# Sixteen gate tiles of the mix made between the steps of inversion, scan and latent attention

## Chip, core and metric

The program runs on one core of a Trainium2 chip. The metric is the device time of one execution in microseconds; the time before is 2737.14 us, the median of three runs (2735.2 to 2739.61).

## What is computed

Two blocks on 256 tokens (16 meta tokens more in the first), width 2048, fp32. The first block is a differential attention and a pooling mixer. The second normalises h, multiplies it by one wide matrix and splits the result in three:

```python
u = rms_norm_2(h, pre_mix_norm[i])
z = u @ w_in[i]
z_rw, z_mla, z_gate = jnp.split(z, (RW_COLS, RW_COLS + MLA_COLS), axis=-1)
y_rw = rwkv7_mixer(z_rw, ...)
y_mla = mla_mixer(z_mla, ...)
g_rw, g_mla = jnp.split(jax.nn.sigmoid(z_gate), 2, axis=-1)
mix = (g_rw * (y_rw @ w_branch_rw[i]) + g_mla * (y_mla @ w_branch_mla[i])) @ w_out[i]
h = h + rms_norm_2(mix, post_mix_norm[i])
```

The gate columns z_gate are 2 x 2048; they depend on u alone. In `rwkv7_mixer` k is multiplied by k_k and divided by the root of its sum of squares per head; `rwkv7_scan` is a recurrence over the tokens for 16 heads of 64. `mla_mixer` is an attention with 8 heads over blocks of 128 queries. After the mix come a feed-forward part (5632 wide, with a convolution) and a gated embedding.

## The kernel before

All activations stand transposed: channels on 128 partitions, tokens along the row, so a 2048-wide tensor is 16 tiles of 128 x 256 (`KT`). Weights stream from DRAM in **slots** of 1 MB (4 x 512 columns on 128 partitions); `SLOTS_OF` gives their order, 393 in all. Four slots are in SBUF at a time (`RAW`). SP asks for slot n as soon as PE is done with slot n-4 (semaphore `slot_used`, `load_weights` L232). Each fp32 product is made of three fp32r products: ScalarE casts a slot to its high part (`split_hi`, L184), VectorE subtracts to get the low part (`split_lo`, L198), each in two halves, and `products` (L208) multiplies high by high, high by low and low by high (L220, L221, L222). `products` waits for `lo_done`. A slot is 48 products of 128 x 128 by 256 columns. A slot is split about two slots before PE uses it. PSUM is eight banks of 512 columns.

Every engine has its order written out by hand; `then_inc` and `wait_ge` on named semaphores hold them together.

The recurrent mixer (`rw_pe` L1060, `rw_act`, `rw_pool`, `rw_dve`) does the heads in two halves b. Per half: 14 slots give k, then w and a (a small slot), r, the gate g (slot n+9, small) and v. VectorE takes each from PSUM with the token shift (`shifted`, L1047 to L1054), sums the logs of the decay in six levels (L1376, L1377), and inverts the norm of k in two reciprocals (L1385, L1387). POOL scales k by k_k and squares it (L1310, L1312). Then come the **grams** (L1127, L1135: 64-wide products of chunks), their masks on VectorE (L1414 to L1425), the **inversion** of a triangular matrix per chunk in five **levels** (L1148 with POOL's mask L1330, ScalarE's copy L1272, then L1157 and L1158, and VectorE's sums L1433, L1434), the **turning** (transposes L1165 and ScalarE's copies, L1173), and the **scan** over four chunks x (L1184, L1190, L1195, L1201, L1202, L1206, L1207), in which `sa` goes through ScalarE (L1282), and the state and `pb` through VectorE (L1458, L1460, L1451). Behind it head sums (L1069) start the group norm while the products of the next part run. The scan stage streams no weights.

`mla_pe` (L1497) does attention per head: `turned` (three transposes of the probabilities), `scores` of head h+2, `values` of head h-1. VectorE takes maxima, divides and takes the low part of the output; ScalarE makes the exponentials.

`mix_pe` (L1745) runs four turns k of 12 slots: 4 for g_rw, 4 for g_mla, 2 for each branch; `mix_dve` multiplies the gates by the norm's factor `rs`, ScalarE takes the sigmoid, VectorE multiplies by the branch and adds both. A gate tile there takes 16 contraction tiles, as everywhere.

## Time and profile before

| what | value |
|---|---|
| median of three runs | 2737.14 us |
| the profiled execution, its own time | 2738.05 us |
| its span, first to last instruction | 2736.3 us |
| mean granted TensorE clock | 0.955 |
| PE busy | 2571.3 us (94%) |
| VectorE / ScalarE / POOL busy | 1653.5 (60%) / 1183.2 (43%) / 144.8 us (5%) |
| chain that ended last: PE / VectorE / ScalarE / POOL | 85% / 8% / 3% / 2% |
| lines L220, L221, L222 in that chain | 26%, 25%, 25% |

PE's busy time counts matmuls whose ends are modelled, so a busy PE is not PE at its peak. The granted clock is 1.00 at 2.4 GHz and 0.50 at 1.2 GHz. An instruction's idle time is put down to whoever released it last.

### The profile page before, as it was taken

Reading aid. Unit: us, or ns where it says so; the run is one execution under the profiler, and the core shown is the slowest. Engines: PE = TensorE matmul, PEld = TensorE weight load, DVE = VectorE, ACT = ScalarE, POOL = GpSimd, SP = SyncE. Lnnn points to the kernel's source line nnn. Section 1 sums busy time; section 2 is a strip of 40 time slices with the busy share of each in tenths; the row PEclk is TensorE's granted clock in tenths of the full one; section 3 lists DMA queues with packets and bytes.
Section 4 is the critical chain, followed back from the end, with each engine's and each line's share of the span. In section 5 each row is a group of like instructions: output and inputs, shape, how many; then the busy total and the mean of one; then the engine's idle time right before and its main releaser. Section 6 shows DMA issues by size and latency. Waiting matters only on the chain.

```text
span 2736.3 us, 52352 instructions
## 1 busy us (share of the span) xinstructions
PE 2571.3 (94%) x22506; PEld 2523.0 (92%) x22506; DVE 1653.5 (60%) x1896; ACT 1183.2 (43%) x1614; POOL 144.8 (5%) x85
## 2 busy tenths in 40 slices
PE   7999999999999887977988999999999999999997
PEld 7999999889999886977977999989999999999997
DVE  6556666565564884483464555548666666666675
ACT  5445455453444631331334333455444444444463
POOL 0000000005200031121000000000000000000000
PEclk9999999899999998797897999999999999999999
DMA  5444434344555430230331555544555555555443
GB/s 222 153 155 145 153 139 149 127 141 173 182 187 190 165 129 14 78 139 2 108 123 68 189 188 188 185 170 170 186 186 184 184 184 184 184 184 184 169 154 123
DMA packets 60053, 420.02 MB, mean 154 GB/s; under 512 B 6512, under 2 KB 8688, under 8 KB 9616
## 3 DMA queue, kind: packets, MB, share of 16 engines
q1 hardware_dynamic: 59712, 417.26, 42.7%
q8 instruction: 112, 1.84, 0.3%
q0 software_dynamic: 208, 0.75, 0.1%
q14 instruction: 21, 0.17, 0.0%
HBM read 415.89 MB, written 2.10 MB: 153 GB/s over the span
## 4 chain that ended last, share of the span: by engine, by line
PE 85%; DVE 8%; ACT 3%; POOL 2%; issue 1%; DMA 0%; DVEq 0%; SPq 0%; POOLq 0%; ACTq 0%
PE banks L220 26%; PE banks L222 25%; PE banks L221 25%; DVE weights_lo_sb L198 2%; PE banks L1158 1%; POOL rw_tile_sb L1310 1%; PE banks L1069 1%; PE banks L1148 1%; PE banks L1157 1%; PE banks L555 1%; PE banks L1544 0%; PE banks L568 0%; PE banks L1195 0%; PE banks L1206 0%; PE banks L1543 0%
## 5 line engine op out<-in xcount | busy, mean ns | idle before, releaser
L220 PE MATMUL banks<-xa_hi_sb,weights_hi_sb 128*128 128x256 f32 (+1 forms) x4864 | 1392.2, 286 | 59.7 <-DVE xa_lo_sb L348 18.9
L222 PE MATMUL banks<-xa_hi_sb,weights_lo_sb 128*128 128x256 f32 (+1 forms) x4864 | 1377.8, 283 | 0.0
L221 PE MATMUL banks<-xa_lo_sb,weights_hi_sb 128*128 128x256 f32 (+1 forms) x4864 | 1375.7, 283 | 0.0
L198 DVE TENSOR_TENSOR weights_lo_sb<-raw_weights_sb,weights_hi_sb 128x1024 fp32r<-128x1024 f32 x786 | 940.3, 1242 | 315.6 <-ACT weights_hi_sb L184 309.3
L184 ACT CAST weights_hi_sb<-raw_weights_sb 128x1024 fp32r<-128x1024 f32 x786 | 779.4, 1047 | 621.9 <-DMA raw_weights_sb<-weights 621.6
L220 PEld LDWEIGHTS banks<-xa_hi_sb,weights_hi_sb 128*128 128x128 f32 x4864 | 923.0, 190 | 66.0 <-issue 39.7
L221 PEld LDWEIGHTS banks<-xa_lo_sb,weights_hi_sb 128*128 128x128 f32 x4864 | 925.6, 190 | 0.5
L222 PEld LDWEIGHTS banks<-xa_hi_sb,weights_lo_sb 128*128 128x128 f32 x4864 | 923.3, 190 | 0.0
L220 PE MATMUL banks<-xb_hi_sb,weights_hi_sb 128*128 128x256 f32 (+1 forms) x688 | 196.5, 286 | 2.7 <-DVE low_flat_sb L1669 1.3
L222 PE MATMUL banks<-xb_hi_sb,weights_lo_sb 128*128 128x256 f32 (+1 forms) x688 | 195.6, 284 | 0.0
L221 PE MATMUL banks<-xb_lo_sb,weights_hi_sb 128*128 128x256 f32 (+1 forms) x688 | 195.5, 284 | 0.0
L220 PE MATMUL banks<-ff_hi_sb,weights_hi_sb 128*128 128x256 f32 x640 | 181.1, 283 | 0.0
L221 PE MATMUL banks<-ff_lo_sb,weights_hi_sb 128*128 128x256 f32 x640 | 180.8, 283 | 0.0
L222 PE MATMUL banks<-ff_hi_sb,weights_lo_sb 128*128 128x256 f32 x640 | 179.4, 280 | 0.0
L220 PEld LDWEIGHTS banks<-xb_hi_sb,weights_hi_sb 128*128 128x128 f32 x688 | 129.9, 189 | 3.7 <-DVE low_flat_sb L1669 1.5
L222 PEld LDWEIGHTS banks<-xb_hi_sb,weights_lo_sb 128*128 128x128 f32 x688 | 130.3, 189 | 0.0
L221 PEld LDWEIGHTS banks<-xb_lo_sb,weights_hi_sb 128*128 128x128 f32 x688 | 130.0, 189 | 0.2
L222 PEld LDWEIGHTS banks<-ff_hi_sb,weights_lo_sb 128*128 128x128 f32 x640 | 121.7, 190 | 0.0
L221 PEld LDWEIGHTS banks<-ff_lo_sb,weights_hi_sb 128*128 128x128 f32 x640 | 120.2, 188 | 0.0
L220 PEld LDWEIGHTS banks<-ff_hi_sb,weights_hi_sb 128*128 128x128 f32 x640 | 119.7, 187 | 0.0
L2106 DVE TENSOR_TENSOR y_sb<-y_sb,banks 128x1024 f32<-128x1024 f32 x40 | 48.8, 1221 | 47.7 <-PE banks L222 47.7
L2057 DVE TENSOR_TENSOR up_gate_sb<-banks,rs_sb 128x1024 f32<-128x1024 f32 x11 | 13.5, 1225 | 84.8 <-PE banks L222 83.1
(380 smaller groups left out, 2080.1 us busy)
## 6 DMA issues: line engine op xcount, KB each, us to landing
raw_weights_sb<-weights SPq DMA_DIRECT2D x393, 1024.0 KB, 4.8
h_sb<-h SPq DMA_DIRECT2D x4, 544.0 KB, 8.2
out<-h_sb SPq DMA_DIRECT2D x4, 512.0 KB, 2.9
...
```

The costliest lines, as they stand in the source:

```text
L184: act.copy(c.w_hi[n % RAW][:, HALVES[x]], c.raw[n % RAW][:, HALVES[x]]).then_inc(c.sem("hi_done"), 1)
L198: dve.tensor_tensor(c.w_lo[n % RAW][:, half], c.raw[n % RAW][:, half], c.w_hi[n % RAW][:, half].bitcast(F32), ALU.subtract).then_inc(c.sem ...
L220: pe.matmul(out, w_hi[:, k, a], x_hi[:, tile, cols], start=begin, stop=False)
L221: pe.matmul(out, w_hi[:, k, a], x_lo[:, tile, cols], start=False, stop=False)
L222: done = pe.matmul(out, w_lo[:, k, a], x_hi[:, tile, cols], start=False, stop=end)
L555: m = pe.matmul(ps[0:b - a, 4 + comp, SCORES_AT[q]:SCORES_AT[q] + b], t["qk"][:, comp, a:b], t["qk"][:, 2 + comp, 0:b], start=True, stop=True)
L1069: m = pe.matmul(ps[:, bank + j // 2, 256 * (j % 2):256 * (j % 2) + 256], ones, src[:, j, :], start=True, stop=True)
L1148: m = pe.matmul(ps[at_[q], g, 64 * (u % 8):64 * (u % 8) + 64], t["lm"][at_[q], u, :], t["yy"][at_[q], u, :], start=True, stop=True)
L1157: pe.matmul(ps[at_[q], 2 + g, cut], t["tt"][at_[q], u, :], t["xx"][at_[q], u, :], start=True, stop=True)
L1158: m = pe.matmul(ps[at_[q], 4 + g, cut], t["xx"][at_[q], u, :], t["tt"][at_[q], u, :], start=True, stop=True)
L1310: m = pool.tensor_scalar(t["kk"][:, j, :], t["k"][:, j, :], c.param("k_k", 4 * b + j), None, ALU.mult)
L2106: dve.tensor_tensor(y, y, out(x), ALU.add).then_inc(S("down_taken"), 1)
```

## The change

**Slots.** The 16 gate tiles of turns 0 and 1 (g = 0 to 15; 4 of g_rw and 4 of g_mla per turn) leave the mix. Each has a slot of its own, all 16 contraction tiles of 128 output channels: 6 slots `kept0` behind the first half of the recurrent mixer, 6 `kept1` behind the second, 4 `kept2` behind the products of latent attention. `mix` has 32 slots instead of 48; there are 393 as before.

**PE.** `kept_products(c, pe, tiles)` issues that many contraction tiles, three products each, and goes on where the last call stopped; they write banks 6 and 7. Its calls: in each half 14 and 6 around the second gram product, 3 and 4 in each of the five levels, 4 behind the transposes, 4 behind L1173's product, 5 at chunk 0, then 4 and 5, 4 and 5, 4 and 6; in attention 12, seven times 7, and 3. That is 96, 96 and 64 tiles. What stood in banks 6 and 7 moves to 0, 1 and 4. In the grams the lower-triangle product comes before that of kt.

**VectorE.** `kept_take` multiplies a finished tile by `rs` into h, in place; low parts of the kept slots stand between levels, chunks and heads. In the normalisation the low parts of n+7, n+8 and n+9 and the one of n+15 come earlier, the second reciprocal later.

**ScalarE.** It squares and scales k instead of POOL, takes n+9's high part before the exponentials, splits the kept slots, and takes the sigmoid of the kept gates in h.

**h.** Before the first take h goes to DRAM (2.2 MB, in SP's queue behind the load of slot 139), and comes back in it behind that of slot 211, when `mixed` is 2.

The core of the diff:

```diff
@@ SLOTS_OF @@
-    ("rw_down", 4), ("rw_half0", 14), ("rw_half1", 14), ("mla_in", 8), ("mla_q", 3), ("mla_kv", 4),
-    ("mix", 48), ("mix_out", 16), ("ffn", FF_STEPS * 12), ("ple", 2), ("ple_gate", 16),
+    ("rw_down", 4), ("rw_half0", 14), ("kept0", 6), ("rw_half1", 14), ("kept1", 6), ("mla_in", 8), ("mla_q", 3), ("mla_kv", 4),
+    ("kept2", 4), ("mix", 32), ("mix_out", 16), ("ffn", FF_STEPS * 12), ("ple", 2), ("ple_gate", 16),
...
+    out_at = (FIRST_SLOT["rw_down"] + 11) // RAW * RAW
+    back_at = (FIRST_SLOT["mix"] + 17) // RAW * RAW
+    loads(RAW, out_at)
+    sp.wait_ge(c.sem("h_ready"), 2 * PAIRS)
+    sp.dma_start(h_aside, c.h[:]).then_inc(c.sem("h_moved"), 16)
+    loads(out_at, back_at)
+    sp.wait_ge(c.sem("mixed"), 2)
+    sp.dma_start(c.h[:], h_aside).then_inc(c.sem("h_moved"), 16)
+    loads(back_at, N_SLOTS)
...
+def kept_products(c, pe, tiles):
+
+    for _ in range(tiles):
+        g, k = c.kept // KT, c.kept % KT
+        n = kept_slot(g)
+        if k == 0 and g >= 2:
+            pe.wait_ge(c.sem("gate_kept"), g - 1)
+        if k % 8 == 0:
+            pe.wait_ge(c.sem("lo_done"), 2 * n + k // 8 + 1)
+        a = slice(P * (k % 4), P * (k % 4) + P)
+        w_hi, w_lo = c.w_hi[n % RAW][:, k // 4, a], c.w_lo[n % RAW][:, k // 4, a]
+        out = c.ps[:, 6 + g % 2, 0:SEQ]
+        pe.matmul(out, w_hi, c.xa[0][:, k, BOTH], start=k == 0, stop=False)
+        pe.matmul(out, w_hi, c.xa[1][:, k, BOTH], start=False, stop=False)
+        m = pe.matmul(out, w_lo, c.xa[0][:, k, BOTH], start=False, stop=k == KT - 1)
...
+def kept_take(c, dve, t, g):
+
+    dve.wait_ge(c.sem("slot_used"), kept_slot(g) + 1)
+    if g == 0:
+        dve.wait_ge(c.sem("h_moved"), 16)
+    dve.tensor_tensor(c.h[:, g, 0:SEQ], c.ps[:, 6 + g % 2, 0:SEQ], t["rs"][:, BOTH], ALU.mult).then_inc(c.sem("gate_kept"), 1)
...
@@ rw_act @@
+        act.wait_ge(S("rw_taken_out"), 3 * b + 1)
+        if b:
+            act.wait_ge(S("rw_out"), 1)
+        for j in range(4):
+            act.activation(t["bon"][:, j, :], t["k"][:, j, :], ACT.Square, scale=c.param("k_k", 4 * b + j))
+        for j in range(4):
+            m = act.activation(t["kk"][:, j, :], t["k"][:, j, :], ACT.Copy, scale=c.param("k_k", 4 * b + j))
+        m.then_inc(S("kk_squared"), 1)
         split_hi(c, act, n + 7)
         act.wait_ge(S("kk_summed"), b + 1)
         act.activation(t["bon"][:], half(2), ACT.Sqrt).then_inc(S("kk_rooted"), 1)
         split_hi(c, act, n + 8)
+        split_hi(c, act, n + 9)
         act.wait_ge(S("logs_ready"), b + 1)
...
-        split_hi(c, act, n + 9)
...
@@ rw_pool @@
-        pool.wait_ge(S("rw_taken_out"), 3 * b + 1)
-        for j in range(4):
-            m = pool.tensor_scalar(t["kk"][:, j, :], t["k"][:, j, :], c.param("k_k", 4 * b + j), None, ALU.mult)
-        st.did(m)
-        pool.tensor_tensor(t["bon"][:], t["kk"][:], t["kk"][:], ALU.mult).then_inc(S("kk_squared"), 1)
...
-        pool.wait_ge(S("grams_taken"), 3 * b + 3)
+        pool.wait_ge(S("grams_taken"), 3 * b + 1)
...
@@ rw_dve @@
-            if level in (1, 4):
-                split_lo(c, dve, n + (7 if level == 1 else 8))
+            if level in (0, 3):
+                split_lo(c, dve, n + (7 if level == 0 else 8))
...
         st.did(dve.tensor_scalar(t["bon"][:], t["bon"][:], 1e-12, None, ALU.max))
+        split_lo(c, dve, n + 9)
         dve.reciprocal(t["bon"][:, 0:2], t["bon"][:, 0:2])
-        split_lo(c, dve, n + 9)
-        st.did(dve.reciprocal(t["bon"][:, 2:4], t["bon"][:, 2:4]))
         split_lo(c, dve, n + 10)
         dve.wait_ge(S("slot_used"), n + 9)
         dve.wait_ge(S("key_scaled"), b + 1)
         shifted(c, dve, st, t, 1, 4, "mu_rkv", 4 * b, t["r"], "rw_taken", n + 11)
+        st.did(dve.reciprocal(t["bon"][:, 2:4], t["bon"][:, 2:4]))
...
+            if level < 3:
+                lo_part(c, dve, n + 17, level - 1)
+            elif level < 5:
+                lo_part(c, dve, n + 18, level - 3)
...
@@ mla_dve @@
+        if h == 2:
+            kept_take(c, dve, t, 12)
+        if h == 4:
+            kept_take(c, dve, t, 13)
+        if h == 7:
+            kept_take(c, dve, t, 14)
+        lo_part(c, dve, n + 2 + h // 2, h % 2)
...
@@ mix_dve @@
     n = FIRST_SLOT["mix_out"]
...
+    dve.wait_ge(S("h_moved"), 32)
     boundary_dve(c, dve, st, t, 3, 5, BOTH, "pre_ffn", {2: n + 18, 4: n + 19})
```

The order on PE from the grams of the first half on, before (`ar_flat` holds the scan's left operands, `rw_tile` all the mixer's tiles, the `y_sb` here the masked triangle):

```order
L1127 MATMUL banks<-ar_flat_sb,rw_tile_sb 64x128 [waits bonus_taken,g_taken,tilde_ready]
L1127 MATMUL banks<-ar_flat_sb,rw_tile_sb 64x128 x31
L1127 MATMUL banks<-ar_flat_sb,rw_tile_sb 64x128 [waits rw_taken]
...
L1135 MATMUL banks<-rw_tile_sb,ar_flat_sb 64x64 [waits grams_taken]
...
L1148 MATMUL banks<-rw_tile_sb,y_sb 64x64 [waits masked_ready,grams_taken]
```

and now (L273 is the first of a kept tile's three products; 14 tiles stand in front of L1171's second group, 6 behind it):

```order
L1171 MATMUL banks<-ar_flat_sb,rw_tile_sb 64x128 [waits bonus_taken,g_taken,tilde_ready]
...
L1181 MATMUL banks<-rw_tile_sb,ar_flat_sb 64x64 [waits rw_taken]
...
L273 MATMUL banks<-xa_hi_sb,weights_hi_sb 128x256 [waits lo_done]
L274 MATMUL banks<-xa_lo_sb,weights_hi_sb 128x256
L275 MATMUL banks<-xa_hi_sb,weights_lo_sb 128x256
...
L1171 MATMUL banks<-ar_flat_sb,rw_tile_sb 64x128 [waits grams_taken]
...
L1199 MATMUL banks<-rw_tile_sb,y_sb 64x64 [waits grams_taken,masked_ready]
```

The lower triangle's product no longer waits for the masks of the first, and PE has 20 tiles of its own between the grams and the first level.

On ScalarE, around the norm of k in the first half, before:

```order
L1244 ACTIVATE rw_tile_sb<-banks,params_sb 128x256 x7
L184 CAST weights_hi_sb<-raw_weights_sb 128x1024 [waits raw_full3]
L184 CAST weights_hi_sb<-raw_weights_sb 128x1024
L1249 ACT_TABLE_LOAD
L1249 ACTIVATE rw_tile_sb<-banks 128x1024 [waits kk_summed]
...
L1252 ACTIVATE rw_tile_sb<-rw_tile_sb 128x1024 [waits logs_ready]
```

and now:

```order
L1303 ACTIVATE rw_tile_sb<-banks,params_sb 128x256 x7
L1310 ACTIVATE rw_tile_sb<-rw_tile_sb,params_sb 128x256 [waits rw_taken_out]
L1310 ACTIVATE rw_tile_sb<-rw_tile_sb,params_sb 128x256 x3
L1312 ACTIVATE rw_tile_sb<-rw_tile_sb,params_sb 128x256 x4
...
L1316 ACTIVATE rw_tile_sb<-banks 128x1024 [waits kk_summed]
...
L1320 ACTIVATE rw_tile_sb<-rw_tile_sb 128x1024 [waits logs_ready]
```

Eight activations with a wait for k now stand ahead of the next high part.

On PE in attention, one head now (L1647 to L1649 transposes, L1640 and L1641 scores, L1656 and L1657 values; before, the same rows without L273 to L275):

```order
L1647 MATMUL banks<-consts_sb,pm_sb 128x128 [waits mla_probs]
L1648 MATMUL banks<-consts_sb,pm_sb 128x128
...
L1641 MATMUL banks<-kpe_sb,late_tmp_sb 128x256
L1656 MATMUL banks<-at_sb,low_flat_sb 128x256 [waits mla_turned_taken]
L1657 MATMUL banks<-at_sb,low_flat_sb 128x128
L273 MATMUL banks<-xa_hi_sb,weights_hi_sb 128x256
```

Seven tiles stand between a head's values and the next wait for probabilities.

## Rows read from the trace of the kernel before

**Rows 1.** Page, part 2: granted clock, tenths, 40 slices of 68.4 us

```profile
PEclk9999999899999998797897999999999999999999
```

**Rows 2.** Windows by stage: us, each engine's busy us (count), clock, DMA share, GB/s

```profile
955.52:1023.72 68.20, 56.46 (x425) 55.34 (x425) 58.45 (x56) 27.98 (x32) 22.61 (x12) 0.90 0.38 139
1023.72:1042.57 18.85, 5.71 (x194) 5.31 (x193) 15.81 (x17) 0.00 (x0) 2.34 (x1) 0.71 0.17 57
1042.57:1076.10 33.53, 30.16 (x897) 29.48 (x897) 12.40 (x19) 5.86 (x10) 9.41 (x4) 0.91 0.02 3
1076.10:1085.13 9.03, 6.06 (x105) 5.55 (x105) 1.20 (x1) 4.43 (x5) 0.00 (x0) 1.00 0.01 2
1085.13:1120.98 35.85, 32.83 (x369) 31.85 (x369) 5.44 (x11) 3.23 (x7) 0.00 (x0) 0.51 0.01 1
1120.98:1132.96 11.98, 11.98 (x64) 11.08 (x65) 3.58 (x3) 4.23 (x4) 0.00 (x0) 0.74 0.02 3
1154.43:1221.36 66.93, 56.37 (x425) 55.16 (x425) 58.48 (x56) 27.46 (x31) 22.62 (x12) 0.90 0.39 143
1240.21:1272.34 32.13, 28.76 (x897) 28.08 (x897) 12.39 (x19) 5.86 (x10) 9.40 (x4) 0.95 0.01 4
1281.37:1315.86 34.49, 31.48 (x368) 30.50 (x368) 5.44 (x11) 3.23 (x7) 0.00 (x0) 0.54 0.01 2
1419.27:1473.86 54.59, 42.80 (x120) 27.26 (x120) 20.73 (x72) 23.86 (x82) 0.00 (x0) 0.56 0.01 5
1550.00:1650.00 100.00, 100.00 (x852) 100.00 (x852) 48.13 (x42) 38.23 (x39) 0.00 (x0) 1.00 0.53 187
```

**Rows 3.** Timeline of PE: start, us, operation, [idle before <- who ended it]

```profile
970.44 0.45 PE L1069 MATMUL banks<-rw_tile_sb,consts_sb 128*128 128x256 f32 x1 [1.89 <-POOL rw_tile_sb L1312]
...
991.12 0.58 PE L1093 MATMUL banks<-lora_hi_sb,weights_hi_sb 128*128 128x256 f32 x1 [7.41 <-DVE weights_lo_sb L198]
...
997.92 0.58 PE L220 MATMUL banks<-xa_hi_sb,weights_hi_sb 128*128 128x256 f32 x1 [2.43 <-DVE y_sb L1047]
...
1042.57 0.37 PE L1148 MATMUL banks<-rw_tile_sb,y_sb 64*64 64x64 f32 x2 [7.88 <-POOL y_sb L1330]
...
1085.13 0.27 PE L1201 MATMUL banks<-sa_sb,rw_tile_sb 64*64 64x64 f32 x1 [0.67 <-ACT sa_sb L1282]
...
1461.13 0.48 PE L1550 MATMUL banks<-consts_sb,pm_sb 128*128 128x128 f32 x1 [1.29 <-DVE pm_sb L1727]
```

**Rows 4.** Timelines of POOL, ScalarE and VectorE, normalisation stretch of the first half

```profile
959.53 8.36 POOL L1310 TENSOR_SCALAR rw_tile_sb<-rw_tile_sb,params_sb 128x256 f32<-128x256 f32 x4 [25.20 <-DVE rw_tile_sb L1054]
...
954.57 3.03 ACT L1244 ACTIVATE rw_tile_sb<-banks,params_sb 128x256 f32<-128x256 f32 x8
...
979.85 1.23 DVE L1381 TENSOR_TENSOR rw_tile_sb<-y_sb,rw_tile_sb 128x1024 f32<-128x1024 f32 x1
...
990.99 3.34 DVE L1387 RECIPROCAL rw_tile_sb<-rw_tile_sb 128x512 f32<-128x512 f32 x1
```

**Rows 5.** Windows: a level, scan at both clocks, two heads' scores, one head

```profile
1063.95:1070.45 6.50, 5.87 (x200) 5.74 (x196) 2.75 (x4) 1.17 (x2) 2.35 (x1) 1.00 0.02 5
1281.90:1283.90 2.00, 2.00 (x47) 2.00 (x46) 0.43 (x1) 0.00 (x0) 0.00 (x0) 1.00 0.03 8
1290.00:1305.00 15.00, 14.22 (x163) 13.87 (x164) 2.79 (x6) 0.95 (x2) 0.00 (x0) 0.50 0.00 1
1419.27:1423.49 4.22, 4.22 (x16) 2.34 (x16) 1.46 (x5) 1.56 (x4) 0.00 (x0) 1.00 0.14 60
1453.91:1461.13 7.22, 5.93 (x15) 3.70 (x16) 2.57 (x9) 2.78 (x11) 0.00 (x0) 0.50 0.00 1
```

**Rows 6.** Page, parts 5 and 6: a low part; DMA issues, KB, us to landing

```profile
L198 DVE TENSOR_TENSOR weights_lo_sb<-raw_weights_sb,weights_hi_sb 128x1024 fp32r<-128x1024 f32 x786 | 940.3, 1242 | 315.6 <-ACT weights_hi_sb L184 309.3
...
raw_weights_sb<-weights SPq DMA_DIRECT2D x393, 1024.0 KB, 4.8
...
h_sb<-h SPq DMA_DIRECT2D x4, 544.0 KB, 8.2
```

236 lines of the change are left out of this document (166 added, 70 removed).

## The prediction

> **What bounds the kernel now.** I first read the clock line of the page's forty slices [rows 1]: TensorE's granted clock is full almost everywhere and dips in slices 13 to 21. There I cut the span into the stages that the change touches [rows 2]: for each half b of the recurrent mixer the normalisation stretch, the gram products, the inversion, the turning, the scan, the stretch behind it; then latent attention; last a plain stretch of the mix. The last of these shows the kernel's usual state: PE busy 100.00 us of 100.00 with 852 products, 117.4 ns each, full clock. There only fewer PE instructions help. In the stages before it PE is idle (13.1 of 18.85 us in the grams) or has the clock at 0.50 (2.4 GHz falls to 1.2 GHz): the scan is at 0.51 and attention at 0.56 on average. The third view, the waits in the PE timeline [rows 3], says who is late: POOL 1.89 us, VectorE's low parts 7.41, its shift of r 2.43, POOL's mask 7.88, ScalarE's copy of sa 0.67 per chunk, VectorE's probabilities 1.29 per head. TensorE is the bound everywhere else, so work moved into those holes is worth its full time, as long as it does not lengthen the chain it is put into.
>
> **The sum, part by part.** It is made against the profiled execution's 2738.05 us (span 2736.3), 0.9 above the median of 2737.14.
>
> *Mix.* 16 slots x 48 products leave it: 768 x 117.4 ns = 90.2 us off the path, -90.2. They come back as 256 kept tiles of 3 products, 0.352 us each at full clock: 96 in each half, 64 in attention.
>
> *Normalisation stretch, twice (68.20 and 66.93 us).* POOL's scaling by k_k took 8.36 us [rows 4] and the square followed; ScalarE makes eight instructions of that size in 3.03 [rows 4], so kk_squared comes at about 962.4 instead of 970.3 and the head sums start right behind the products, 1.9 us sooner. The square root then ends at 971.5, high part n+8 at 973.5, its low part at 974.9; two scan levels (a pass of 1.24 [rows 6] and a small copy each, 1.4 and 1.1) and the subtraction end at 978.6, where they ended at 979.85 + 1.23 [rows 4]. Low part n+9 no longer stands behind the first reciprocal (3.35 us) and n+9's high part is cast before the exponentials: with the clamp (0.7) it is ready at 981.65, just as PE finishes n+8 (968.55 + 1.6 of head sums + 2 x 5.63 = 981.4). The 7.41 us wait goes. The small product of that slot then ends at 984.4. Next late is the shift of r, behind one reciprocal and low part n+10: 981.65 + 3.35 + 2.35 + 1.22 = 988.5, so the products that started at 997.92 start at 988.5. What is queued behind: the second reciprocal and four operations now precede low part n+12, first half at 1001.2 where PE would want it at 999.8; 1.4 us of stall. And PE is idle for 4.1 us, after which the clock is half for a while, as after the 5 us hole before the inversion; some 2.5 us, in which the stall is hidden. So -9.4 + 1.1 in the first half, -1.2 less in the second, which had less half clock: -8.3 and -7.6, sum -15.9. Bounds: -4 (only POOL's waits go, twice 1.9) to -21 (no clock loss).
>
> *Grams to level 1, twice 18.85 us.* VectorE's masks start 2.3 us sooner (low part n+15 goes ahead of the shift of v); the lower product needs no mask first; POOL's mask needs only the first signal. From the start of the grams: the shift of v ends at 4.3, three masks of 1.2 at 7.9, POOL's mask (2.34 [rows 2]) at 10.4, three more passes of VectorE at 11.6. PE does bt grams 1.9, lower 1.0, 14 tiles 4.9 to 7.8, kt grams at 8.0, 6 tiles to 12.0, and starts level 1 at 12.0. -6.85 each, -13.7, with 20 tiles inside.
>
> *Inversion (33.53 and 32.13 us).* A level is 6.50 us with 5.87 busy [rows 5]; its own starts use 5.7. Seven tiles (2.46) make it 8.2, above VectorE's 2.76 + 1.24 [rows 6] + 0.35 for the level's updates, a low half and a take. Four of those and 6.3 for the last: 39.1. +5.6 +7.0 = +12.6, with 35 tiles inside each.
>
> *Turning and x = 0 (9.03 each).* 13 tiles (4.6) where PE is idle 2.97 us now, less what their last matmuls overlap: 10.3. +1.3 each, +2.5.
>
> *Scan (35.85 and 34.49 us).* Without its waits (0.67 four times and 0.92) 32.3 us of small products at half clock. At full clock the rows give 47 of them in 2.00 us against 163 in 15.00 [rows 5], a ratio of 0.46; where they hit the same quadrant it is nearer 0.6. I take 17.5 us (bounds 14.9 and 19.4). Add 28 tiles, 9.9, and 0.9: 28.3. -7.55 and -6.2, sum -13.7. VectorE's chain from ds_done to p_taken, with a low half in it, is 4.4 us and just fits PE's 4.4 to the end of the kept four.
>
> *Behind the scan (11.98, and as much in the second half).* 3.2 us of half clock goes each time: -6.4.
>
> *Latent attention (54.59 us).* A head is 7.22 us, half clock, 1.29 of it idle [rows 3, 5]. The chain is transposes and scores, then VectorE's 2.57 busy with 0.3 of hand-over. At full clock two heads' scores took 4.22 [rows 5], so transposes and scores are 2.45. VectorE gets a low half (1.24) and, every second head, a take (0.35) into the chain: 4.1 to 4.5, beside which PE has values and 7 tiles, 3.3. A head is then 6.55 to 6.95, and with 12 tiles ahead of the first the stage ends at 1474.5: +0.6. I add 2 for half-clock spells, since PE still rests 0.8 per head: +2.6.
>
> *h aside and back.* 2 x 2.2 MB in the queue of the weights. h's four loads (0.54 MB) landed in 8.2 us, a slot's 1.0 MB in 4.8 [rows 6]; DMA is busy 0.53 of 5.63 us per slot, 3.0 us, so h is 6.4 us of transfer. A slot is asked for three slots (16.9 us) before its use and needs 4.8 + 2.3 + 2.5: 7.3 to spare. The store falls where ScalarE's table and sine work already delays the slots. I take 0; bounds 0 and +10. If that cover were gone PE would wait on raw_full.
>
> *Switches.* Some 60 changes between small and kept products, at most 0.1 us each: +3. Half-clock spells in the scan, where a stretch of small products alone lasts 5 us: +3.
>
> Sum: -90.2 -15.9 -13.7 +12.6 +2.5 -13.7 -6.4 +2.6 +3 +3 = **-116.2**, which gives 2738.05 - 116.2 = 2621.9.
>
> The weak place is the clock. The row from 1290 to 1305 has PE busy 14.22 of 15.00 us at 0.50: the scan's products, one quarter of the array each, never brought the clock back, nor did attention's, while the inversion's pairs of quadrants did within 6 us. So a full queue isn't enough by itself; whether the kept products, 128 x 128, keep the clock up there is what most of the sum's risk hangs on. The Trainium skill (TensorE: Matmul & The Clock Gate, Part 1: The HAM clock gate) says the gate follows how busy PE has been and that sustained activity releases it. Read so, the scan of before should have been at 2.4 GHz, and the rows contradict it. By that rule a change that closes nearly every hole has full clock throughout, and the sum would be 2617.
>
> **The rivals.**
> *A, the forecast:* full clock with short spells, 2622. For it: a third of each chunk and each head is now of the very products that run at full clock all over the kernel, most of the idle time before the falls is gone, and the inversion holds full clock with no product in it. Its own range is 2600 to 2655. Chance 0.68.
> *B, half clock stays in scan and attention.* For: both rows at 0.50, with PE 95% and 82% busy. Price: small products 14.8 x 2; 56 tiles and attention's at 0.70 us instead of 0.35, where a head becomes 5.9 + 4.9 = 10.9 us; the stretches behind: 29.5 + 19.7 + 30 + 6.4 = 86, less the 5 allowed: 2703. Chance 0.13.
> *C, the reordered chain or the transfers give less.* Low parts or the second reciprocal hold PE again (+9), or a slot lands late behind h (+10), together about 2641. Against: the arithmetic above leaves them 0 to 7 us of room. Chance 0.15.
> *D, slower.* One mechanism: the clock is half in the inversion too, since kept groups stretch the chain and the small products thin out. Then 256 tiles cost 0.352 more (90), levels 5.87 x 9.4 more (55), scan 30, turning 10, the rest 11: 196 more, 2818. It turns the sign when about six tenths of that happens. Against: that stage is at 0.91 and 0.95 now, with no kept product in it. Chance 0.04, of which 0.01 lands within 0.2%.
> That the tiles aren't made in the holes at all is ruled out by PE's order.
>
> **The numbers.** The likeliest case gives 2622. The range takes A's bounds, C, and the near part of B (half clock in one of the two stages, 2655 to 2680): 2602 to 2680. Anything within 0.2% (5.5 us, about what a measurement of this kernel can tell from no change) would need D halfway: 0.01. Faster 0.96 (A, B, C), slower 0.03.
>
> **What would show it.** The mix shorter by 90 us; the wait of PE on low part n+9 gone, with a new one of some 4 us for VectorE's shift of r; level 1 starting 12.0 us behind the first gram; levels of 8.2 us; clock near 1.00 in the scan and chunks of 8.7 us; heads of 6.6 to 7 us with VectorE as releaser. Wrong would be: 0.50 in the scan or in attention, chunks near 16 us, heads near 11, waits of ScalarE's casts on raw_full around the two moves of h that reach PE, or a new wait on gate_kept.

## The result, and the profile after

The changed kernel takes **2639.51 us** (median of 4 runs, 2637.62 to 2639.89); the kernel before, run beside it, 2737.04. The ratio is 0.9639, 95% interval 0.9625 to 0.9653: 97 us less, inside the range that was given (2602 to 2680), 17.5 us above the forecast of 2622.0. The profiled execution took 2637.62 us with a span of 2635.7 (before: 2738.05 and 2736.3), so 100.6 us of span to explain where the sum had 116.2. Of all executions behind the medians of this document one, of the kernel with smaller blocks, took 3105.62 us at a mean clock of 0.748; it moves that median by 0.01 us, and the ratio is made without it.

The page's granted clock, 40 slices, of after; it answers to [rows 1]:

```profile
PEclk9999999999999999999999999999999999999999
```

The dips in slices 13 to 21 are gone; the mean clock rose from 0.955 to 0.986. The windows by stage of after, cut at the same instructions as [rows 2] (us, busy us and count of each engine, clock, DMA share, GB/s):

```profile
954.40:1014.80 60.40, 55.20 (x425) 54.46 (x425) 57.04 (x58) 33.30 (x42) 14.26 (x7) 0.92 0.43 156
1014.80:1028.61 13.81, 12.26 (x254) 11.71 (x253) 13.52 (x14) 0.00 (x0) 3.35 (x1) 1.00 0.35 114
1028.61:1070.64 42.03, 42.03 (x1001) 40.16 (x1002) 25.20 (x30) 11.53 (x16) 9.49 (x4) 1.00 0.18 66
1070.64:1081.44 10.80, 10.80 (x146) 10.26 (x144) 2.88 (x3) 6.23 (x7) 0.00 (x0) 1.00 0.06 8
1081.44:1113.93 32.49, 30.77 (x453) 29.21 (x453) 10.18 (x18) 5.13 (x9) 0.00 (x0) 1.00 0.21 77
1113.93:1122.94 9.01, 9.01 (x64) 8.62 (x65) 4.67 (x4) 4.23 (x4) 0.00 (x0) 1.00 0.20 76
1144.40:1205.00 60.60, 54.71 (x424) 53.77 (x424) 56.68 (x58) 32.67 (x41) 12.71 (x7) 0.94 0.44 157
1218.82:1260.85 42.03, 42.03 (x1002) 40.16 (x1003) 25.20 (x30) 11.53 (x16) 9.49 (x4) 1.00 0.18 66
1271.64:1304.16 32.52, 30.80 (x454) 29.24 (x453) 10.18 (x18) 5.12 (x9) 0.00 (x0) 1.00 0.22 77
1404.80:1411.72 6.92, 6.92 (x17) 3.63 (x17) 1.46 (x5) 4.95 (x11) 0.00 (x0) 0.56 0.08 34
1404.80:1463.51 58.71, 53.34 (x313) 42.81 (x313) 31.02 (x84) 31.40 (x90) 0.00 (x0) 0.91 0.17 60
```

Read against [rows 2], this is the ledger, in us of span, both halves together, with the forecast's term beside each:

| stage | measured | forecast |
|---|---|---|
| up to the normalisation | -1.1 | 0 |
| normalisation | -14.1 | -15.9 |
| grams to level 1 | -10.1 | -13.7 |
| inversion | +18.4 | +12.6 |
| turning | +3.5 | +2.5 |
| scan | -5.3 | -13.7 |
| behind the scan | -5.7 | -6.4 |
| attention | +4.1 | +2.6 |
| the rest, with the mix | -90.3 | -90.2 |
| switches, and clock spells in the scan, put into no stage | in the stages | +6 |
| sum | -100.6 | -116.2 |

The large term is exact: "the rest" is what is left of the spans, and the stretch behind attention alone went from 1262.4 us (2736.3 - 1473.86) to 1172.2 (2635.7 - 1463.51), 90.2 less. The scan has its granted clock at 1.00 where it had 0.51, and PE is busy through all of the inversion. What is off is small per place and repeated: every level, every chunk.

The waits of after, from the timeline of PE (start, us, operation, idle before and who ended it):

```profile
988.51 0.58 PE L220 MATMUL banks<-xa_hi_sb,weights_hi_sb 128*128 128x256 f32 x1 [5.20 <-DVE y_sb L1091]
...
1028.61 0.59 PE L1199 MATMUL banks<-rw_tile_sb,y_sb 64*64 64x64 f32 x13 [1.55 <-DVE rw_tile_sb L1493]
...
1095.30 0.88 PE L1247 MATMUL banks<-ar_flat_sb,state_sb 64*64 64x64 f32 x15 [0.49 <-DVE rw_tile_sb L1527]
...
1404.80 0.46 PE L1640 MATMUL banks<-y_sb 128*128 128x128 f32 x2 [1.25 <-ACT low_flat_sb L1711]
...
1423.78 0.33 PE L1647 MATMUL banks<-consts_sb,pm_sb 128*128 128x128 f32 x1 [0.90 <-DVE pm_sb L1834]
```

Of [rows 3] the 1.89 us for POOL's square, the 7.41 for low part n+9 and the 7.88 for POOL's mask are gone. In their place stand the 5.20 us for the shift of r (forecast 4.1) and 1.55 ahead of level 1 (forecast 0), each once per half.

Two timelines of after show what the sum had not priced. The first is that of PE at the edges of the block of 14 kept tiles:

```profile
1017.64 0.38 PE L273 MATMUL banks<-xa_hi_sb,weights_hi_sb 128*128 128x256 f32 x1
1017.86 0.28 PE L274 MATMUL banks<-xa_lo_sb,weights_hi_sb 128*128 128x256 f32 x1
1017.98 0.28 PE L275 MATMUL banks<-xa_hi_sb,weights_lo_sb 128*128 128x256 f32 x1
...
1022.55 0.28 PE L275 MATMUL banks<-xa_hi_sb,weights_lo_sb 128*128 128x256 f32 x1
1022.76 1.98 PE L1171 MATMUL banks<-ar_flat_sb,rw_tile_sb 64*64 64x128 f32 x64
```

Within a block one product starts 0.12 us after another; the second starts 0.22 after the first, and the first 64 x 64 product 0.21 after the last 128 x 128 one. That is 0.1 us at each edge, 5.12 us for a block that is 4.93 at 117.4 ns each.

The second, of VectorE and then of POOL, lies a little later, ahead of level 1:

```profile
1022.65 1.23 DVE L1491 TENSOR_TENSOR rw_tile_sb<-rw_tile_sb,masks_sb 128x1024 f32<-128x1024 f32 x1
1023.80 3.40 DVE L1492 TENSOR_TENSOR rw_tile_sb<-rw_tile_sb,masks_sb 128x1024 f32<-128x1024 f32 x1
1027.23 1.23 DVE L1493 TENSOR_TENSOR rw_tile_sb<-rw_tile_sb,masks_sb 128x1024 f32<-128x1024 f32 x1
...
1022.76 3.35 POOL L1400 TENSOR_TENSOR y_sb<-rw_tile_sb,masks_sb 128x1024 f32<-128x1024 f32 x1 [37.68 <-DVE rw_tile_sb L1489]
```

L1492 has the shape and operands of its neighbours and takes 3.40 us instead of 1.23. POOL's mask runs from 1022.76 to 1026.11; VectorE's pass ends 1.1 us after that. POOL's own pass takes 3.35 where one alone took 2.34 [rows 2].

### The profile page after: what moved, and what is told of

Its sections match the earlier page's. It is cut to its first block, busy times and chain, and to the rows that moved or that the text cites. A ratio compares the mean times of both kernels' runs of the same rounds, so it can differ in the third digit from the quotient of the medians.

```text
span 2635.7 us, 52257 instructions
## 1 busy us (share of the span) xinstructions
PE 2523.7 (96%) x22506; PEld 2478.7 (94%) x22506; DVE 1653.6 (63%) x1908; ACT 1187.7 (45%) x1630; POOL 128.7 (5%) x75
## 4 chain that ended last, share of the span: by engine, by line
PE 87%; DVE 9%; ACT 2%; issue 1%; POOL 1%; DMA 0%; DVEq 0%; SPq 0%; POOLq 0%; ACTq 0%
PE banks L220 26%; PE banks L222 25%; PE banks L221 25%; DVE weights_lo_sb L198 2%; PE banks L273 1%; PE banks L274 1%; PE banks L275 1%; PE banks L1199 1%; PE banks L1212 1%; PE banks L1211 1%; PE banks L599 1%; PE banks L612 1%; PE banks L1113 0%; POOL sums_sb L990 0%; PE banks L1641 0%
## 5 line engine op out<-in xcount | busy, mean ns | idle before, releaser
L220 PE MATMUL banks<-xa_hi_sb,weights_hi_sb 128*128 128x256 f32 (+1 forms) x4608 | 1319.0, 286 | 66.4 <-DVE xa_lo_sb L392 19.0
L222 PE MATMUL banks<-xa_hi_sb,weights_lo_sb 128*128 128x256 f32 (+1 forms) x4608 | 1305.7, 283 | 0.0
L221 PE MATMUL banks<-xa_lo_sb,weights_hi_sb 128*128 128x256 f32 (+1 forms) x4608 | 1303.8, 283 | 0.0
L220 PEld LDWEIGHTS banks<-xa_hi_sb,weights_hi_sb 128*128 128x128 f32 x4608 | 873.8, 190 | 72.7 <-issue 40.9
L221 PEld LDWEIGHTS banks<-xa_lo_sb,weights_hi_sb 128*128 128x128 f32 x4608 | 876.6, 190 | 0.4
L222 PEld LDWEIGHTS banks<-xa_hi_sb,weights_lo_sb 128*128 128x128 f32 x4608 | 874.6, 190 | 0.0
L273 PE MATMUL banks<-xa_hi_sb,weights_hi_sb 128*128 128x256 f32 x256 | 77.9, 304 | 0.0
```

The source lines that it names most:

```text
L220: pe.matmul(out, w_hi[:, k, a], x_hi[:, tile, cols], start=begin, stop=False)
L221: pe.matmul(out, w_hi[:, k, a], x_lo[:, tile, cols], start=False, stop=False)
L222: done = pe.matmul(out, w_lo[:, k, a], x_hi[:, tile, cols], start=False, stop=end)
L273: pe.matmul(out, w_hi, c.xa[0][:, k, BOTH], start=k == 0, stop=False)
```

## The experiments

Theory at this point: (1) the clock is held by the 128 x 128 tiles that now stand among the small products; (2) the shortfall is the edges of the blocks, POOL and VectorE in each other's way, the holes ahead of attention, and small products in the scan slower than taken. Each had a rival. The medians below are of 5 runs (smaller blocks: 6). The kernels ran on several chips; each ratio is to the kernel before on the same chip, which took 2736.8 to 2739.9 us there. A ratio has an interval of about +-0.0013, or 3.6 us, so differences of 3 to 6 us between kernels are read from the stages of the traces, which repeat to some hundredths of a us, and the medians only have to agree with them.

### The kept tiles in one block ahead of the scan

```diff
             m.then_inc(S("turned_rw"), 1)
-        kept_products(c, pe, 4)
+        kept_products(c, pe, 41)
...
-        kept_products(c, pe, 4)
...
-                kept_products(c, pe, 4)
...
-            kept_products(c, pe, 5 if x < 3 else 6)
...
         split_lo(c, dve, n + 19)
+        kept_take(c, dve, t, 6 * b + 3)
```

> The 37 products groups of kept tiles that stand behind the turning and inside the scan are moved in one block ahead of the scan; nothing is added or left out. Theory 1 (interleaved 128x128 products hold the clock at full; the small products alone let it fall): the scan runs at the granted clock of before, about 0.5, and takes again some 35 us per half instead of 32.5 with tiles in it; the stretch behind it again 12 instead of 9. Sum of turning, block and scan 54 to 56 us instead of 43.3 per half, so 27 to 32 us more than the changed kernel in all: about 2669. Theory 2 (the tiles only fill holes; the clock is full because the chain ahead was mended): clock 1.00 in the scan, 19.7 us of small products and some 10 us of waits, 6.6 us more per half: about 2653. If both the clock and the holes are worth nothing: 2640.

Measured: 2676.81 us, ratio 0.9779 (0.9766 to 0.9791), 37 us above the changed kernel. Windows of its trace, the block and then the scan:

```profile
1076.00:1086.00 10.00, 10.00 (x87) 10.00 (x86) 1.56 (x2) 0.00 (x1) 0.00 (x0) 1.00 0.40 128
1086.00:1096.00 10.00, 7.66 (x130) 7.25 (x130) 0.00 (x0) 3.38 (x4) 0.00 (x0) 1.00 0.50 188
1096.00:1106.00 10.00, 9.33 (x112) 9.14 (x111) 2.34 (x3) 0.95 (x2) 0.00 (x0) 0.53 0.01 2
1106.00:1116.00 10.00, 9.17 (x103) 8.64 (x100) 3.33 (x6) 0.95 (x2) 0.00 (x0) 0.50 0.01 2
```

The block is 14.7 us of uninterrupted full-width products at 1.00 and ends at 1089.35. Behind it come small products and two waits, of 1.11 and 1.22 us, still at 1.00; some 7 us behind the block, between 1096 and 1097, the granted clock falls, and it stays at 0.50 with PE busy nine tenths of the time. The scan took 37 us in each half, without its tiles, where it takes 32.5 with 28 of them. So the clock of the scan does not come from the mended chain ahead of it, as theory 2 had it: the same tiles do the same work in both kernels, and where they stand decides. What the run does not separate is how they hold the clock among the small products, by their width or by filling the waits of 0.67 us and more that the scan has without them; both are gone or back together. For the width speaks that the scan's small products do not hold or bring back the clock where they have no wait among them: from 1094.91 to 1103.74 PE is busy throughout here, the clock falls in that stretch and stays at 0.50, and in the kernel before it stays at 0.50 through 10 busy us (1095.14 to 1105.09). The cost was 5 us above the top of my range.

### Smaller blocks, the same products

```diff
                 m.then_inc(S("tm_done"), 1)
-            kept_products(c, pe, 3)
+                kept_products(c, pe, 1 + g)
...
                 m.then_inc(S("xy_done"), 1)
-            kept_products(c, pe, 4)
+                kept_products(c, pe, 1 + 2 * g)
```

> In each of the ten levels of the inversion the 3 kept tiles behind the first products are given as 1 and 2, the 4 behind the second as 1 and 3: 20 blocks more, the same products. Theory 1 (each block of kept tiles costs 0.2 us for the two changes between 64x64 and 128x128 products): 4 us more, level 9.2 us instead of 8.8, about 2643.5. Theory 2 (a change costs nothing, what is missing in the inversion is VectorE and ScalarE being late): 0, or a little less than 0, since the first group's copy gets more cover.

Measured: 2644.37 us, ratio 0.9659 (0.9647 to 0.9672). The inversion of the first half, its window:

```profile
1028.31:1073.91 45.60, 45.60 (x1001) 41.72 (x1002) 25.09 (x30) 11.54 (x16) 10.17 (x4) 1.00 0.17 62
```

PE has no idle time in it, executes what it executed in 42.03, and takes 3.57 us longer; in the second half the two kernels differ by 3.58. That is **0.36 us per block**, not 0.2. (The medians differ by 4.9 us and the profiled spans by 6.6, where the two windows give 7.2; this is within the interval.) The missing part is on the side of the small products: two groups of 32 take 1.07 and 1.08 us where 64 in one went in 2.01. Theory 1 had the mechanism and too small a price.

### h moved twice

```diff
     sp.dma_start(h_aside, c.h[:]).then_inc(c.sem("h_moved"), 16)
+    sp.wait_ge(c.sem("h_moved"), 16)
+    sp.dma_start(h_aside, c.h[:]).then_inc(c.sem("h_moved"), 16)
...
     sp.dma_start(c.h[:], h_aside).then_inc(c.sem("h_moved"), 16)
+    sp.wait_ge(c.sem("h_moved"), 48)
+    sp.dma_start(c.h[:], h_aside).then_inc(c.sem("h_moved"), 16)
```

> h is moved aside twice and brought back twice, each second move behind the first: two moves of 8.2 us more on the queue of the weights. Theory 1 (the moves lie in stretches where the weights are loaded ahead): 0 to 1 us, about 2640. Theory 2 (part of what the change fell short by is the two moves, which hold weight tiles back): what one pair costs is added again, 5 to 16 us, 2645 to 2656, with TensorE or ScalarE waiting for raw weights.

Measured: 2645.66 us, ratio 0.9663 (0.9651 to 0.9676), 6 us more: the second pair is not hidden. The waits of PE in the 100 us around the store, first of the changed kernel, then of this one (us in total, times, longest):

```profile
PE banks L220 <- DVE xa_lo_sb L392: 6.4, 1, 6.4
PE banks L220 <- DVE weights_lo_sb L198: 3.2, 2, 1.7
PE banks L1138 <- DVE weights_lo_sb L198: 0.2, 1, 0.2
```

```profile
PE banks L220 <- DVE xa_lo_sb L396: 6.4, 1, 6.4
PE banks L1142 <- DVE weights_lo_sb L198: 2.1, 1, 2.1
PE banks L220 <- DVE weights_lo_sb L198: 1.9, 2, 1.5
```

With two moves in a row a weight tile comes too late (2.1 us there, and 2.5 us on a low part behind the load back). These waits are, net, 3 of the 9 us between the spans of the two profiled executions; the granted clock is also lower behind the store (0.83 against 0.91 from 940 to 960 us, 0.93 against 1.00 from 960 to 985), and the rest was not followed. With one, the changed kernel has no wait in either place that the kernel before does not have, though each move took 11 us to land. So the moves cost nothing, but by a cover that one more of them uses up; my expectation that the second would also be free was wrong.

### The mask of level 1 by VectorE

```diff
         dve.tensor_tensor(t["yy"][:], t["yy"][:], mask("eye"), ALU.add)
+        dve.tensor_tensor(t["lm"][:], t["ll"][:], mask("level1"), ALU.mult).then_inc(S("masked_ready"), 1)
...
-        for level in range(1, 6):
-            if level > 1:
-                pool.wait_ge(S("tm_done"), 2 * (5 * b + level - 1))
+        for level in range(2, 6):
+            pool.wait_ge(S("tm_done"), 2 * (5 * b + level - 1))
```

PE's wait for the identity in xx at level 1 goes with it; the wait on the last masks, ahead of the second products, stays.

> The mask of level 1 is made by VectorE between its two additions of the identity, instead of by POOL beside them. Theory 1 (VectorE's pass took 3.40 us instead of 1.22 because POOL worked beside it): that pass takes 1.2 us, the wait of 1.56 us ahead of level 1 goes in both halves, 3.1 us less: about 2636.5. Theory 2 (the pass is slow for a reason of its own): VectorE has one pass more, the pass stays at 3.4 us, TensorE waits about 2 us behind the first products of level 1 instead of 1.56 ahead of them: 0 to 1 us more, 2640.

Measured: 2635.17 us (2630.72 to 2639.46), ratio 0.9627 (0.9615 to 0.9640). The pass and the window from the grams to level 1 in its trace:

```profile
1025.47 1.22 DVE L1489 TENSOR_TENSOR rw_tile_sb<-rw_tile_sb,masks_sb 128x1024 f32<-128x1024 f32 x1
```

```profile
1015.33:1027.52 12.19, 12.19 (x254) 11.68 (x253) 11.90 (x14) 0.00 (x0) 0.00 (x0) 1.00 0.26 93
```

The pass is 1.22 us, the wait is gone, 12.19 instead of 13.81 us and 12.18 instead of 13.82 in the second half: 3.3 us, as theory 1 had it. VectorE does one pass more and ends sooner.

This kernel's five times spread by 9 us and follow the mean clock: 0.986 at 2630.7 and 2631.0, 0.982 at 2639.5. Its profiled execution ran the first two heads' scores at full clock, the changed kernel's at half (0.50 from 1405.6 to 1415.7), behind the same three holes of 1.3 us each. A spell of half clock behind such holes is there in one execution and not in another. So of the 6.7 us between the two spans 4.5 are that spell (54.18 us of attention instead of 58.71) and not this edit.

### Six tiles in the holes ahead of attention

```diff
         if x >= 5:
+            if x == 6:
+                kept_products(c, pe, 3)
             pe.wait_ge(S("up_taken"), x + 1)
...
+    kept_products(c, pe, 3)
     pe.wait_ge(S("q_roped"), 1)
...
-        kept_products(c, pe, 7 if h else 12)
+        kept_products(c, pe, 7 if h else 6)
```

> Of the 12 kept tiles of the first head 3 are given while TensorE waits for the last of the up products to be evacuated and 3 while it waits ahead of the first scores; the first head keeps 6. Theory 1 (attention begins at half clock because of the holes of 1.3 and 2.0 us ahead of it): the scores of the first two heads take 4.2 us instead of 6.9, the first head's tiles run at full clock, and 2.1 us of them stand in holes: 5 to 7 us less, about 2633.5. Theory 2 (scores and transposes alone lower the clock, whatever stands ahead): the scores still take 6.9 us, 2 us less: about 2637.5.

Measured: 2632.32 us, ratio 0.9621 (0.9608 to 0.9634). The window of the first two heads' scores:

```profile
1405.86:1410.08 4.22, 4.22 (x17) 2.41 (x17) 1.46 (x5) 3.43 (x6) 0.00 (x0) 1.00 0.14 60
```

4.22 us against 6.92, and 51.1 instead of 57.4 us from the first scores to the last values. That looks like theory 1, but one execution does not show it: the kernel with VectorE's mask had the holes open and full clock too, and took 52.9 us there. The tiles in the holes are worth the 1.8 us between 52.9 and 51.1; the other 4.5 are the spell. Whether filled holes prevent it is a matter of counting: of the ten profiled executions of this study with the holes open three have full clock in the first scores (the kernel before among them, [rows 5]) and seven half; of the four with tiles in them all have full clock. That speaks for theory 1 and is no proof. (The holes are 1.32, 1.32 and 1.25 us in the changed kernel's trace, not 1.3 and 2.0 as I had expected; here the last two are 0.26 and 0.18.)

### The shift of r first, and POOL out of its way

```diff
         split_lo(c, dve, n + 9)
-        dve.reciprocal(t["bon"][:, 0:2], t["bon"][:, 0:2])
         split_lo(c, dve, n + 10)
...
         shifted(c, dve, st, t, 1, 4, "mu_rkv", 4 * b, t["r"], "rw_taken", n + 11)
+        split_lo(c, dve, n + 12)
+        dve.reciprocal(t["bon"][:, 0:2], t["bon"][:, 0:2])
         st.did(dve.reciprocal(t["bon"][:, 2:4], t["bon"][:, 2:4]))
```

Low part n+13 moves to where n+12 was. The second kernel has this too, and one wait on POOL:

```diff
         pool.wait_ge(S("exps_ready"), b + 1)
+        pool.wait_ge(S("lo_done"), 2 * (FIRST_SLOT[f"rw_half{b}"] + 12) + 2)
         pool.tensor_tensor(t["kt"][:], t["k"][:], t["tt4"], ALU.mult)
```

> VectorE makes the shift of r ahead of both reciprocals (before: between them), low part n+12 ahead of them and n+13 behind the bonus. Theory 1 (what is late there is VectorE's queue; the wait of TensorE for the shift of r, 5.2 us, is half reciprocal): the wait falls to some 2 us, 3.2 us less per half, and the clock need not fall to half behind it, another 0 to 3 us per half: 6.4 to 12 us less, about 2630. Theory 2 (the time only moves to the next late thing, the sums of the bonus and the low parts behind both reciprocals): a new wait of 2 to 3 us ahead of the bonus sums, 0 to 2 us less: 2638.

> As the one with the shift of r first, and POOL's two products with the exponentials wait until low part n+12 is made, so that they stand beside the reciprocals instead of beside low part n+10. Theory 1 (POOL slows VectorE's two-operand passes, 4.04 us instead of 2.35 there, and not its reciprocals, 3.35 us with and without POOL): low part n+10 takes 2.35 us, the shift of r comes 0.7 to 1.7 us sooner per half, 1.4 to 3.4 us less than without it. Theory 2 (the slowness of that pass is not POOL's): no difference.

Measured: 2638.25 us, ratio 0.9644 (0.9631 to 0.9657) for the first, nothing gained; **2628.37 us, ratio 0.9609** (0.9595 to 0.9622) with POOL's wait. The first kernel's low part n+10, POOL's two products, and PE behind them:

```profile
980.82 5.95 DVE L198 TENSOR_TENSOR weights_lo_sb<-raw_weights_sb,weights_hi_sb 128x1024 fp32r<-128x1024 f32 x2 [1.11 <-ACT weights_hi_sb L184]
...
980.00 2.40 POOL L1392 TENSOR_TENSOR rw_tile_sb<-rw_tile_sb,y_sb 128x1024 f32<-128x1024 f32 x1 [14.03 <-ACT y_sb L1323]
982.36 3.32 POOL L1393 TENSOR_TENSOR rw_tile_sb<-rw_tile_sb,y_sb 128x1024 f32<-128x1024 f32 x1
...
987.97 0.58 PE L220 MATMUL banks<-xa_hi_sb,weights_hi_sb 128*128 128x256 f32 x1 [5.03 <-DVE y_sb L1091]
```

And the second kernel's:

```profile
981.09 2.36 DVE L198 TENSOR_TENSOR weights_lo_sb<-raw_weights_sb,weights_hi_sb 128x1024 fp32r<-128x1024 f32 x2 [1.10 <-ACT weights_hi_sb L184]
...
992.02 3.35 DVE L1462 RECIPROCAL rw_tile_sb<-rw_tile_sb 128x512 f32<-128x512 f32 x1
...
992.28 2.42 POOL L1393 TENSOR_TENSOR rw_tile_sb<-rw_tile_sb,y_sb 128x1024 f32<-128x1024 f32 x1 [26.04 <-DVE weights_lo_sb L198]
...
984.65 0.39 PE L220 MATMUL banks<-xa_hi_sb,weights_hi_sb 128*128 128x256 f32 x1 [1.43 <-DVE y_sb L1091]
```

Neither theory of the first kernel was right (that theory 2 named 2638 is luck: the wait ahead of the bonus sums did not come). The reciprocal that was moved away was VectorE's cover while POOL worked: without it VectorE first waits 1.11 us for ScalarE's high part, and the pass that POOL holds up is the critical one, 5.95 us instead of 2.36. Beside the reciprocals POOL's products cost VectorE nothing (3.35 us as alone) and take 2.4 us each. With 1.43 us of idle time instead of 5.20 the clock also stays full there. The gain over the first is about 10 us by the medians, well above the 3.4 I gave it at most; but 4.5 of the 10.4 us between the two profiled spans are the spell ahead of attention, which this execution happened not to have with its holes open. Against the changed kernel attention starts 7.1 us sooner, and that is what the edit gives. Part of the gain moved on: the grams to level 1 take 16.3 us instead of 13.8 in each half, 1.9 of it a new wait for the shift of v.

The Trainium skill (SBUF — State Buffer, Who interferes with whom) says that a VectorE operation with both inputs in SBUF and a GpSimd operation that reads SBUF exclude each other, and that the later one waits for the whole of the earlier. The rows agree: VectorE's SBUF passes end 1.1 us after POOL's, and the first pass of a shift, which reads one input from PSUM, takes 1.22 us beside a POOL product in the trace of the changed kernel, as alone:

```profile
1140.27 1.22 DVE L1091 TENSOR_TENSOR y_sb<-banks,rs_sb 128x1024 f32<-128x1024 f32 x1 [2.02 <-issue]
...
1140.79 2.38 POOL L1583 TENSOR_TENSOR y_sb<-rw_tile_sb 128x1024 f32<-128x1024 f32 x1
```

By that rule L1492 would be 1026.11 - 1023.80 + 1.23 = 3.5 us; it took 3.40.

### k scaled and squared by POOL again

```diff
-            act.activation(t["bon"][:, j, :], t["k"][:, j, :], ACT.Square, scale=c.param("k_k", 4 * b + j))
...
+            m = pool.tensor_scalar(t["kk"][:, j, :], t["k"][:, j, :], c.param("k_k", 4 * b + j), None, ALU.mult)
+        st.did(m)
+        pool.tensor_tensor(t["bon"][:], t["kk"][:], t["kk"][:], ALU.mult).then_inc(S("kk_squared"), 1)
```

> The part of the change that has ScalarE scale and square k is undone: POOL does it again, all else stays. By the forecast's working the squares come 8 us later than now, TensorE waits 1.9 us ahead of the head sums and the whole chain to the shift of r is later by 5 us, of which the next late part hides some: 4 to 10 us more, 2644 to 2650. Rival (the gain of that stretch comes from the reordered low parts alone): within 1 us of the changed kernel, 2639.5.

Measured: 2645.94 us, ratio 0.9667 (0.9654 to 0.9680), 6.4 more by the medians. The waits of PE in its two normalisation stretches:

```profile
PE banks L220 <- DVE y_sb L1091: 10.1, 2, 5.3
PE banks L1113 <- POOL rw_tile_sb L1381: 5.3, 2, 3.4
```

The waits for the squares come back (1.9 and 3.4 us) and the rest of the chain is shifted by them; the wait for the shift of r stays as it was. ScalarE's eight instructions are 3.4 us in two groups, where [rows 4] gave 3.03.

### The normalisation part alone, on the kernel before

The same edits of POOL, ScalarE and VectorE as in the change, in the kernel before; no tile is moved, the grams stay.

> The kernel before with the normalisation part of the change alone: ScalarE scales and squares k, low parts and high parts n+7 to n+10 earlier, the second reciprocal behind the shift of r. No tile is moved, the grams stay as they were. Theory 1 (that stretch gives what the cuts of the two traces show, 7.8 and 6.3 us, by itself): 14 us less than before, 2723, the wait on low part n+9 (7.4 us) gone and one of some 5 us for the shift of r in its place. Rival (its gain needs the rest of the change, since the kernel's later stages take up what comes early): 0 to 5 us less, 2732 to 2737.

Measured: 2728.15 us, ratio 0.9956 (0.9943 to 0.9970): 12 us less than the 2739.87 of before on that chip (interval 8 to 16). The waits of PE there:

```profile
PE banks L1148 <- POOL y_sb L1331: 15.8, 2, 7.9
PE banks L1135 <- DVE rw_tile_sb L1416: 10.5, 2, 5.3
PE banks L220 <- DVE y_sb L1047: 10.5, 2, 5.3
```

The wait on low part n+9 is gone and 10.5 us for the shift of r have come, as in the changed kernel; the waits around the grams are untouched. About an eighth of the whole gain (by the interval a twelfth to a sixth) is this reorder and needs no moved tile.

### What helped, together

The mask by VectorE, the tiles ahead of attention, and the shift of r with POOL's wait, in one kernel:

> The changed kernel with the three edits that helped alone: the mask of level 1 by VectorE, 3 + 3 tiles in the holes ahead of attention, the shift of r ahead of the reciprocals with POOL's products beside these. Theory 1 (each mends a different wait; alone they gave 4, 7 and 11 us): 19 to 22 us less, about 2618. Rival (the shift of v and VectorE's masks behind it become the bound of the grams once PE comes sooner, and take one of the gains): 2624 to 2628.

Measured: 2622.00 us, ratio 0.9572 (0.9559 to 0.9585): 18 us below the changed kernel, near theory 1's 19 to 22 and outside the rival. The grams to level 1 take 14.60 us here, not the 12.19 of the mask alone:

```profile
1014.58 0.64 PE L1181 MATMUL banks<-rw_tile_sb,ar_flat_sb 64*64 64x64 f32 x28 [1.90 <-DVE y_sb L1091]
```

PE comes sooner and waits for the shift of v, behind two low parts. What the rival describes is there, but it is no loss of this kernel: with the shift of r and POOL's wait alone the stage already took 16.3 us, and the mask gives its 1.7 here as well. What the 4, 7 and 11 us had counted three times is the spell ahead of attention, 4.5 us that was missing in each of the three profiled executions. So the next kernel makes low part n+15 later:

```diff
-        split_lo(c, dve, n + 15)
         dve.wait_ge(S("slot_used"), n + 14)
...
         dve.tensor_tensor(t["ll"][:], lower, mask("after"), ALU.mult).then_inc(S("grams_taken"), 1)
+        lo_part(c, dve, n + 15, 0)
...
         dve.wait_ge(S("grams_taken"), 3 * b + 3)
+        lo_part(c, dve, n + 15, 1)
```

> The kernel with the three edits together, and low part n+15 is made in halves behind the masks of the grams, instead of ahead of the shift of v: TensorE waits 1.9 us there for VectorE, and the tile group that reads n+15 comes 16 tiles later. Theory 1 (VectorE's order is what is late): the wait for the shift of v goes, level 1 starts 1.5 to 2 us sooner in each half, 3 to 4 us less than the three edits together, about 2618.5. Theory 2 (VectorE is full from there to the masks of level 1, so its order does not matter): the wait moves to the masks, 0 to 1 us less, 2621.5.

Measured: 2621.55 us, ratio 0.9577 (0.9564 to 0.9590): no difference that can be told. Its windows from the grams to level 1, and of the inversion:

```profile
1010.36:1022.70 12.34, 12.27 (x254) 11.69 (x253) 12.24 (x15) 0.00 (x0) 0.00 (x0) 1.00 0.25 89
1022.70:1066.10 43.40, 42.38 (x1003) 40.27 (x1003) 26.71 (x33) 11.53 (x16) 9.49 (x4) 1.00 0.21 75
```

2.26 us were won, and 1.37 given back in the inversion (42.03 us without this edit): 0.49 is a wait for VectorE's masks ahead of level 1's second products, 0.52 are waits for its sums ahead of level 2, and 0.36 stays open. VectorE is busy 12.24 of the 12.34 us of the first window, and order no longer helps it. The last kernel adds to this one fewer blocks:

```diff
-            kept_products(c, pe, 3)
+            kept_products(c, pe, 3 if level == 1 else 0)
...
-            kept_products(c, pe, 4)
+            kept_products(c, pe, 4 if level == 1 else 7)
```

> As the one with low part n+15 later, and in levels 2 to 5 the 3 and the 4 kept tiles are given as one block of 7 behind the second products: 8 blocks less, the same products. Theory 1 (a block costs 0.35 us, as the 20 added ones showed): 2.8 us less than without it. Rival (the 3 tiles covered ScalarE's copy of the first products, or kept the clock): a wait of 0.5 us or more ahead of the second products of each level, or a clock below 1.00 in the inversion: 0 to 4 us more.

Measured: **2618.54 us, ratio 0.9567** (0.9554 to 0.9580), on the same chip 3.0 us less than without the edit. The inversion:

```profile
1022.90:1064.95 42.05, 41.02 (x1002) 39.69 (x1002) 27.78 (x34) 11.54 (x16) 9.45 (x4) 1.00 0.22 76
```

Level 1 starts at 1022.92, so the stage is 42.03 us: 1.37 us less in each half for four blocks, 0.34 us per block, and the clock stays at 1.00. The price of a block in the inversion is the same measured by adding and by taking away. This is the fastest kernel of the study, 21 us below the changed one.

## Why the prediction was right, and where it was off

- **The mix, -90.2.** Measured -90.2 behind attention. A full queue at full clock gives back 117.4 ns per product that is taken out.
- **The clock in scan and attention, the risk of the forecast.** Right: 1.00 in the scan, 0.91 over attention. That the kept products hold it up there is shown by the block ahead of the scan; that it is their full width that does it, and not the waits they fill, is not shown. Rivals B and D did not come about: chunks of 9.4 to 10.0 us (forecast 8.7), not 16.
- **Normalisation, -15.9.** Measured -14.1. The wait on low part n+9 went and one for the shift of r came, as worked out; 5.2 us of it instead of 4.1. The step that failed took low part n+10 as 2.35 us, and beside POOL's products it was 4.04. The price stood in the trace of the kernel before, where low part n+9 takes 5.89 us beside POOL's two products L1322 and L1323 (984.35 to 989.98):

```profile
985.17 5.89 DVE L198 TENSOR_TENSOR weights_lo_sb<-raw_weights_sb,weights_hi_sb 128x1024 fp32r<-128x1024 f32 x2
```

  The sum has a slip as well: -8.3 with 1.2 less for the second half is -7.1, not -7.6.
- **Grams, -6.85 each.** Measured -5.0. The step "three more passes of VectorE at 11.6" took 1.2 us for a pass that had 3.40 beside POOL's mask; without POOL there the stage took 12.19 where the forecast had 12.0. In the kernel before VectorE was done (1039.94) when POOL's mask began (1040.08); it was the change that set them side by side.
- **Inversion, a level of 8.2 us.** It was 8.8. The sum took seven tiles as 2.46 and the small products as 5.7; the two blocks cost 0.7 by the rate that the experiments give, and that is the whole of this miss.
- **Switches, some 60 of at most 0.1 us each, +3.** This is the step that failed most, in number and in price. There are 42 blocks next to 64 x 64 products; four of them (behind level 5 and behind the transposes) stand where the shape changed before, so 38 are new, with two changes each. At the 0.35 us per block of the inversion this is an estimate of 13.3 us, 10 more than the 3 of the sum; for the scan and the grams that price was not measured by itself, and the misses of the inversion, the grams and the scan above and below contain it. I had bounded an edge where no row of before had one, and should have kept a wider bound. The other +3, for half-clock spells in the scan, was not needed.
- **Scan, 17.5 us of small products.** Measured 19.7 in each half, just above the upper bound that I gave (19.4). The 28 tiles take 11.0 us with their edges instead of 9.9, and the waits are 1.7 instead of 0.9 (two chunks also wait 0.49 and 0.31 us for VectorE). The ratio of full to half clock was mis-sized: the small products from the second chunk's state update to the third's `sa` took 9.95 us before (1095.14 to 1105.76, without 0.67 of wait) and take 5.91 now, 0.59, where 17.5 of 32.3 is 0.54.
- **Attention, +2.6.** Measured +4.1, with the first scores at half clock. In the trace of the kernel with VectorE's mask that spell is missing, and the stretch from the first scores to the last values takes 52.9 instead of 57.4 us. A head is 6.0 to 6.8 us with VectorE as releaser (forecast 6.6 to 7), so here the mechanism was right and the 2 us for half-clock spells were too few for this execution and too many for the other.
- **h aside, 0 with bounds 0 and +10.** Right by its waits, and the doubled move shows how near the cover is to its end.

Rival C named the size (2641) with partly the right causes: PE did not wait for transfers, but the reordered chain gave 5.4 us less than taken (1.8 in the normalisation, 3.6 in the grams).
